# The prompt turned in chunks of 256 tokens, and the sample's outputs with the states as the stationary side, in one decoder kernel

## What is computed

```python
def ret_chunk(S, inp):
    ...
    o_inter = jnp.exp(b)[..., None] * jnp.einsum('bhtk,bhkv->bhtv', q, S)
    ...
    o = o_inter + jnp.einsum('bhts,bhsv->bhtv', A, v)
...
def mixer(h, pos, w_in, w_a2, b_a, gn_gla, gn_ret, w_out, s_gla, s_ret):
    ...
    o_r = head_rmsnorm(o_r, gn_ret, h.dtype) * jax.nn.silu(g_r)
    out = jnp.concatenate([o_a, o_r], axis=-1) @ w_out
...
def trunk(...):
    for l in range(DEPTH):
        x = x + 0.5 * rmsnorm(swiglu(rmsnorm(x, n[0]), w1_gu[l], w1_down[l]), n[1])
        m, S_a, S_r = mixer(rmsnorm(x, n[2]), pos, ...)
        x = x + rmsnorm(m, n[3])
        x = x + 0.5 * rmsnorm(swiglu(rmsnorm(x, n[4]), w2_gu[l], w2_down[l]), n[5])
```

## Time and profile before

| | |
|---|---|
| time, median of 3 runs | 2246.22 us (2245.95 to 2246.39) |
| profiled execution | 2246.0 us, span 2244.2 us |
| PE busy / PEld busy | 2217.3 us (99%) / 2189.0 us (98%) |
| DVE, ACT, POOL busy | 818.0, 822.1, 940.4 us |
| DMA | 197.60 MB, mean 88 GB/s |
| first product of the FFN | 19.7 us after the start of the span |

### The profile page before, as it was taken

One profiled execution on the slowest core, in us unless ns is written; L12 is line 12 of the kernel. 1 busy time (PEld: TensorE's weight loads), 2 busy tenths in 40 slices (PEclk: granted clock), 3 DMA queues, 4 the chain that ended last, 5 costly groups with the idle time before them and its releaser, 6 DMA issues.

```text
span 2244.2 us, 43741 instructions
## 1 busy us (share of the span) xinstructions
PE 2217.3 (99%) x17875; PEld 2189.0 (98%) x17875; DVE 818.0 (36%) x1150; ACT 822.1 (37%) x1445; POOL 940.4 (42%) x776
## 2 busy tenths in 40 slices
PE   8999999999999999999999999999999999999998
PEld 8999999999989999999999999999999899999998
DVE  5222200577367422220162222006863783222102
ACT  4333333442344433232353333335424453333333
POOL 3444444443315444444544444444432244444442
PEclk9999999999999999999999999999999999999999
DMA  6323222332234222323323322232221343322222
GB/s 172 91 84 90 76 85 85 89 84 76 67 83 141 76 84 84 93 69 91 112 70 90 88 84 74 87 95 78 82 75 49 94 130 94 92 86 82 78 88 74
DMA packets 382590, 197.60 MB, mean 88 GB/s; under 512 B 8868, under 2 KB 381400, under 8 KB 382360
## 3 DMA queue, kind: packets, MB, share of 16 engines
q1 hardware_dynamic: 365680, 186.93, 28.9%
q10 hardware_dynamic: 16808, 9.20, 1.4%
HBM read 186.80 MB, written 9.31 MB: 87 GB/s over the span
## 4 chain that ended last, share of the span: by engine, by line
PE 95%; DVE 3%; ACT 1%; issue 0%; DMA 0%; ACTq 0%; DVEq 0%
PE ps L544 88%; PE ps L719 1%; PE ps L879 1%; DVE x L1502 1%; DVE y L1496 1%; DVE xs_lo L1439 1%; PE ps L820 0%; PE ps L793 0%; PE ps L896 0%; PE ps L799 0%; PE ps L571 0%; PE ps L826 0%; ACT xs_hi L1069 0%; PE ps L760 0%; PE ps L822 0%
## 5 line engine op out<-in xcount | busy, mean ns | idle before, releaser
L479 POOL TENSOR_TENSOR w_lo<-raw,w_hi 128x512 fp32r<-128x512 f32 (+1 forms) x708 | 877.5, 1244 | 1150.5 <-ACT w_hi L1096 1150.4
L544 PE MATMUL ps<-xs_hi,w_hi 128*128 128x288 f32 (+1 forms) x3616 | 767.3, 289 | 4.4 <-DVE xs_lo L1439 4.2
L544 PE MATMUL ps<-xs_hi,w_lo 128*128 128x288 f32 (+1 forms) x3616 | 765.3, 288 | 0.0
L544 PE MATMUL ps<-xs_lo,w_hi 128*128 128x288 f32 (+1 forms) x3616 | 762.9, 288 | 0.0
L1096 ACT ACTIVATE w_hi<-raw 128x512 fp32r<-128x512 f32 (+1 forms) x708 | 409.9, 584 | 956.8 <-PE ps L544 956.0
L544 PEld LDWEIGHTS ps<-xs_hi,w_hi 128*128 128x128 f32 x3616 | 588.4, 189 | 11.0 <-DVE xs_lo L1439 6.2
L544 PEld LDWEIGHTS ps<-xs_lo,w_hi 128*128 128x128 f32 x3616 | 588.0, 189 | 0.2
L544 PEld LDWEIGHTS ps<-xs_hi,w_lo 128*128 128x128 f32 x3616 | 584.8, 188 | 0.0
L1460 DVE TENSOR_TENSOR tmp<-ps,rstd_pre 128x544 f32<-128x544 f32 x88 | 63.8, 725 | 630.2 <-PE ps L544 614.0
L544 PE MATMUL ps<-h_hi,w_lo 128*128 128x256 f32 x1272 | 267.2, 289 | 0.0
L544 PE MATMUL ps<-h_lo,w_hi 128*128 128x256 f32 x1272 | 266.1, 288 | 0.0
(11 more groups left out here) (214 smaller groups left out, 1874.1 us busy)
## 6 DMA issues: line engine op xcount, KB each, us to landing
raw<-in_w_gu_dram SPq DMA_DIRECT2D x176, 512.0 KB, 3.8
raw<-in_w_in_dram SPq DMA_DIRECT2D x56, 512.0 KB, 3.7
raw<-in_w_down_dram SPq DMA_DIRECT2D x64, 384.0 KB, 3.4
raw<-in_w_down_dram SPq DMA_DIRECT2D x64, 320.0 KB, 3.2
raw<-in_w_out_dram SPq DMA_DIRECT2D x16, 512.0 KB, 3.8
ret_state<-in_state_ret_dram SPq DMA_DIRECT2D x8, 512.0 KB, 6.0
out_dram<-ret_state ACTq DMA_DIRECT2D x8, 512.0 KB, 5.2
x_tok<-in_x_prompt_dram SPq DMA_DIRECT2D x4, 512.0 KB, 6.3
```

The costliest lines, as they stand in the source:

```text
L479: pool.tensor_tensor(lo, raw[:, u, k0:k0 + n, :], hi.bitcast(F32), ALU.subtract)\
L544: mm = pe.matmul(bank_part(bank, a), w, v[:, kx, TOK[a]], start=(start and n == 0), stop=(stop and n == 2))
```

## The change

It has two parts that do not touch each other.

**The start.** The prompt is loaded by chunks of 128 tokens. SP loads chunks 0 and 1, and ACT's queue loads chunks 2 and 3 once chunks 0 and 1 have landed. The sample's load comes last of ACT's first loads and has its own semaphore. PE turns chunks 0 and 1 (16 transposes), two tiles into one bank, runs the 7 products of `keep_clock_up`, and begins `first_three`. After the first four tiles of part 0 it turns the sample's tokens and chunks 2 and 3 (`turn_others`, 24 transposes), and goes on. DVE's copies and ACT's splits follow this order.

**The sample in the mixer's tail.** The state of a batch element becomes the stationary side (128 columns), and its 4 queries the moving side. The outputs then have the head's values on partitions and the 32 tokens as columns, so that they need not be turned. `mask_queries` becomes `decay_queries` (one product on POOL). The sums of squares become a product with a matrix of ones on PE (`sample_sums`, at k = 3), the root is taken on 256 columns, and DVE gates the outputs while that goes on (`gate_sample`). `back(l, S)` is gone.

```diff
 @block.sync
-            for i in range(X_PARTS):
-                cols = slice(i * D // X_PARTS, (i + 1) * D // X_PARTS)
-                sp.dma_start(x_tok[:, 0:NCH, cols], x_prompt[0, :, cols].rearrange("(c p) d -> p c d", p=P))\
-                    .then_inc(x_loaded[i], 16)
+            for c_ in range(NCH // 2):
+                sp.dma_start(x_tok[:, c_, :], x_prompt[0, c_ * P:(c_ + 1) * P, :]).then_inc(x_loaded[c_], 16)
...
-            def mask_queries(l):
+            def decay_queries(l):
 
                 pool.wait_ge(tables_loaded, 16)
-                wait(pool, o_ready, l, NCH - 2)
                 pool.sem_inc(mask_begun, 1)
...
+                pool.tensor_tensor(q_ret_s.rearrange("p h (b t) -> p h b t", t=DS),
+                                   q_r[:, :, TP:T].rearrange("p h (b t) -> p h b t", t=DS),
+                                   q_decay.broadcast_to([P, HR, NS, DS]), ALU.mult).then_inc(q_masked.sem, 1)
...
+            def turn_inputs(j, a):
+
+                for d in (2 * j, 2 * j + 1):
+                    for c_ in range(2 * a, 2 * a + 2):
+                        at = (d % 2 * 2 + c_ % 2) * P
+                        mm = pe.transpose(ps[:, TURN_BANKS[a][j], at:at + P], x_tok[:, c_, d * P:(d + 1) * P], ident)
+                mm.then_inc(x_turned, 1)
+
+            def turn_others():
+
+                pe.wait_ge(sample_loaded, 16)
+                pe.wait_ge(vec_ready, 1)
+                for d in range(KD):
+                    mm = pe.transpose(ps[:, 1, d * TS:(d + 1) * TS], x_tok[0:TS, NCH, d * P:(d + 1) * P], ident[0:TS, 0:TS])
+                mm.then_inc(x_turned, 1)
+                for c_ in range(NCH // 2, NCH):
+                    pe.wait_ge(x_loaded[c_], 16)
+                pe.wait_ge(x_ready.sem, KP)
+                for j in range(KP):
+                    turn_inputs(j, 1)
+
             def first_three(l, q, g0):
 
                 for a in range(2):
                     for half, k0, n in half_units(KD):
+                        if (l, q, a, half) == (0, 0, 0, 1):
+                            turn_others()
...
-                    keep_clock_up(WARM_UP, 6)
+                    keep_clock_up(WARM_UP, 2)
...
                 for h in heads:
-                    pe.matmul(place(h), a_gla_s[:, h % 2, h // 2, :] if h < HG else a_ret_s[:, h - HG, :],
-                              v_gla_s[:, h, :] if h < HG else v_ret_s[:, h - HG, :], start=True, stop=False)
+                    pe.matmul(place(h, slice(0, TS)), v_gla_s[:, h, :] if h < HG else v_ret_s[:, h - HG, :],
+                              a_gla_s[:, h % 2, h // 2, :] if h < HG else a_ret_s[:, h - HG, :], start=True, stop=False)
                 for b in range(NS):
+                    at = slice(b * DS, (b + 1) * DS)
                     for h in heads:
                         if h < HG:
                             rows = slice(h % 2 * DKG, (h % 2 + 1) * DKG)
-                            queries, state = q_gla_s[rows, h // 2, b * TS:(b + 1) * TS], gla_state[rows, h // 2, b, :]
+                            state, queries = gla_state[rows, h // 2, b, :], q_dec[rows, h // 2, TP + at.start:TP + at.stop]
                         else:
-                            queries, state = q_ret_s[:, h - HG, b * TS:(b + 1) * TS], ret_state[:, h - HG, b, :]
-                        mm = pe.matmul(place(h), queries, state, start=False, stop=(b == NS - 1))
+                            state, queries = ret_state[:, h - HG, b, :], q_ret_s[:, h - HG, at]
+                        mm = pe.matmul(place(h, at), state, queries, start=False, stop=(b == NS - 1))
                 if heads[-1] == HA - 1:
                     mm.then_inc(o_ready.sem, 1)
+
+            def sample_sums(l):
+
+                wait(pe, k_low, l, 0)
+                wait(pe, o_sq, l, S)
+                pe.matmul(ps[:, 3, 0:SW], ones, sq[:, 0, 0:SW], start=True, stop=True).then_inc(o_ms.sem, 1)
...
-                        if k0 + k == BACK_S_AT:
-                            back(l, S)
+                        if k0 + k == SUMS_S_AT:
+                            sample_sums(l)
...
-                    if l == 0 and q == 0 and 1 <= k <= 4:
-                        split_high(g, (k - 1) % 2, FULL_KT, ((k - 1) // 2,))
+                    if l == 0 and q == 0 and k % 4 == 3:
+                        for u in range(2):
+                            split_high(g, u, FULL_KT, (k // 4,))
...
+            def square_sample(l):
+
+                wait(act, o_ready, l, S)
+                for gla in (True, False):
+                    o = act.activation(sample_out(gla, sq_sample), sample_out(gla), ACT.Square)
+                o.then_inc(o_sq.sem, 1)
+
+            def root_sample(l):
+
+                wait(act, o_ms, l, S)
+                act.activation(sq[:, 1, 0:SW], ps[:, 3, 0:SW], ACT.Ln, bias=eps, scale=1.0 / DV).then_inc(o_log.sem, 1)
+                wait(act, o_log, l, S)
+                act.activation(sq[:, 1, 0:SW], sq[:, 1, 0:SW], ACT.Exp, scale=-0.5).then_inc(o_root.sem, 1)
...
+            for c_ in range(NCH // 2, NCH):
+                act.wait_ge(x_loaded[c_ - NCH // 2], 16)
+                act.dma_start(x_tok[:, c_, :], x_prompt[0, c_ * P:(c_ + 1) * P, :]).then_inc(x_loaded[c_], 16)
...
+            def gate_sample(l):
+
+                v = v_t[:, :, TP:T]
+                wait(dve, o_sq, l, S)
+                for gla in (True, False):
+                    o = dve.tensor_tensor(sample_out(gla, v), sample_out(gla), sample_out(gla, g_t[:, :, TP:T]), ALU.mult)
+                o.then_inc(sample_gated.sem, 1)
+                wait(dve, sample_gated, l, 0)
+                wait(dve, o_root, l, S)
+                dve.tensor_tensor(v, v, rstd_sample, ALU.mult)\
+                   .then_inc(o_gated.sem, 1)
...
+            take_inputs(0, 0)
+            take_inputs(1, 0)
+            for j in range(KP):
+                pre_low(0, 0, 0, 2 * j)
+                pre_low(0, 0, 0, 2 * j + 1)
+                if j + 2 < KP:
+                    take_inputs(j + 2, 0)
```

110 lines of the change are left out of this document (44 added, 66 removed).

## The result

The changed kernel takes 2272.15 us (median of 4 runs, 2271.84 to 2272.44), the kernel before 2246.3 in the same call (2245.95 to 2246.87). The ratio is 1.0114, interval 1.0102 to 1.0127: slower by 25.9 us, where the prediction had 2244.3 and called any loss over 0.2% unlikely. The profiled execution took 2272.44, its span is 2270.6.

The account below looks back on a forecast made before the run. PE, busy 99% of the span, was taken as the bound. From 2246.0 us, the start's -1.9 and the tail's +0.1 gave 2244.2, stated as 2244.3; the range for 8 in 10 was 2240.0 to 2246.8.

Parts of the forecast that it names:

- Number of products: the same: Mixer's tail: each layer keeps 64 instructions for retention heads and 32 pairs for GLA heads.
- Sum of a layer: +0.05: Mixer's tail: all its cost changes together add 0.05 us a layer, +0.1 for two layers.
- So the load now sets the pace at 112 ns: Tail's state products: loading 128 columns sets 112 ns each, adding 96 x 0.003 = 0.3 us a layer.
- Rivals 1 and 2: Tail: 128-column loads cost 66 ns (2235.4 us, 6 in 100), or retention products cost 60 (2237.5, 5 in 100).
- Rival 4: Tail: a state's load does not overlap the product before it, up to 188 ns each, 2259 us; 7 in 100.
- The terms of `back(l, S)` and `sample_sums`: Tail: dropping `back` saves 0.61 us and some 0.1 of wait, `sample_sums` adds 0.43; net -0.25 a layer.
- At nothing I cost the rest: Tail: the squares, root, gating, splits and masking on other engines add no time to PE, size zero.
- POOL's masking was off PE's path already: Tail: changing POOL's masking of the sample's queries costs PE nothing, size zero.
- 1.0 to 2.7: Start: range of the net gain in us, with 1.9 as the expected value.
- (b): Start: the warm-up `keep_clock_up`, 3.9 us with PE slow at first, holds the first product until 15.05.
- (a): Start: the split weights hold the first product; POOL's second low part ends at 14.65.
- 0.08 for slower: Whole kernel: chance of being slower by over 0.2%.

Follow-up runs that it names:

- the run with six fillings: Changed tail, first pair moving 128 columns, the rest 32, six unread fp32r products behind each state product from head 2: 2327.81 us, ratio 1.0361.
- the run with the clock kept: Changed tail, start of the kernel before, 32 masked query columns read four times so each state product moves 128: 2247.47 us, ratio 1.0005.
- The form before with 4 columns: Kernel before, queries still stationary, each product moving only 4 of its state's 128 columns, the other work left out: 2246.01 us, ratio 0.9998.
- the start alone: Kernel before with only the changed start (loads, input transposes, order of `first_three`), mixer's tail as before: 2245.07 us, ratio 0.9994.
- two fillings of 256 columns: Changed kernel plus two unread fp32r products of 256 columns behind each state product from head 2 on: 2330.15 us, ratio 1.0375.

## Why the prediction was wrong

**The step that failed** is the sum of the tail. "Number of products: the same" and the costs behind it took every duration at the clock of the rows of before, and "Sum of a layer: +0.05" names nothing that could change it. The layers measured +12.7 and +13.7. Of these, 0.56 each is the wait for VectorE, nearly all the rest the clock. The mechanism was in no rival: the moved columns of the sample's products fell from 128 to 4, and TensorE ran at half the clock, for L894 and also for what came behind it (18 products of L540 in 4.05 instead of 2.13, as the run with six fillings shows them).

**The pace of the load was right.** "So the load now sets the pace at 112 ns": the first pair, still at 1.00, took 1.88 for 16 pairs, 112 ns each and the change of kind, and the run with the clock kept took 1.98 for 16 of 128 columns. Rivals 1 and 2, that loads cost 60 to 66, are out. The form before with 4 columns shows what would be cheap: loads of 32 columns, 59 ns for each instruction even at half the clock. Rival 4 gave a time on the right side, 2259, for a reason that did not occur: at full clock the pace was at most 12 ns over the 112 (124 in the run with 128 columns). A reader who took only its sign would have been right by accident.

**The terms of `back(l, S)` and `sample_sums`** (-0.61 and +0.43; with the 0.1 of wait they make -0.28, where the prediction writes -0.25) can't be read in the changed kernel, where L902 took 0.85 at half the clock; in the run with 128 columns L901 took 0.43 as said, and the tail as a whole came out 0.4 a layer longer than before (L916 at 681.04 against 680.67, start unchanged).

**At nothing I cost the rest** held for ScalarE and VectorE behind the sums, but not for GpSimd: "POOL's masking was off PE's path already" was true of the masking, yet its wait and its clearing held the weight splits back from VectorE's decay. Price 0.56 a layer.

**The start** was mis-sized in one term. Chunk 1 was to land at 1.7 + 5.8 = 7.5 and landed at 8.87, between 8.02 and 8.91 in the other runs where it came last. Its load had the size of the row that it was taken from, but the shape of whole rows, with the weights issued behind it on the same queue; which of the two delayed it is not shown. The vectors' table came at 7.22 as said (7.3), the transposes took 3.65 (3.4), the warm-up 3.96 (3.9), and so the products began at 16.60 instead of 15.2. The transposes took 2.51 of it back (2.6). Net 0.6 in that execution and 1.0 in the profile of the start alone, whose runs stood 1.5 under the kernel before, inside the noise: the low end of 1.0 to 2.7 or under it. That range was itself wider than its terms give, which is 1.3 to 2.3 for products that begin between 15.8 and 14.8. Of the two conditions, (b) was the binding one in the changed kernel, as the prediction had it: the low parts of (a) were done at 15.99, 0.6 ahead of the warm-up's end. They were late too, by 1.3 against the 14.65 that it gave, so cutting the warm-up alone could have gained 0.6 at most here.

**The range and the chances** followed the failed step: 0.08 for slower rested on a load sticking out, and the clock had no case of its own, though the prediction itself reads both levels out of the earlier trace rows for the start.

## What to carry to other kernels

When an edit swaps the sides of a product, cost two things: the columns loaded, which set the pace here once they exceeded the columns moved, and the columns moved per us, which here decided whether the clock stayed at half. Read the granted clock for each stretch, not for the span: 0.986 over the whole hid two stretches at 0.50 worth some 25 us. An instruction that moves repeated columns nobody needs can be the cheaper one, and taking a wait off an idle engine moves all that is queued behind it, here into another engine's way.

## What the runs showed of the hardware

- TensorE busy for 27.00 of 27 us, without a gap, ran at 0.50; the same loads with 128 instead of 4 or 32 moving columns ran at 1.00. 64 columns gave runs from 2254 to 2274.
- The loss outlasts its cause: with the changed tail the 18 output products behind it still took 4.05 instead of 2.13, and two fillings of 256 columns at half the clock did not bring it back in 50 us.
- The form with 128 columns is not safe in every execution: in two of the profiled runs that had it only for the first pair, this pair took 3.58 and 3.45 instead of 1.99 in one of the layers (clock 0.57 from 653 to 657 in the first). In both the fall came just ahead of the pair, and the clock was back at 1.00 by its end.
- At half the clock a head of 16 products with loads of 128 columns takes 3.50, with loads of 32 columns 0.94, both with 4 moving.
- VectorE's decay of 512 columns takes 0.68 alone, 0.94 and 1.25 beside GpSimd's subtraction of 512.
